# Idle TensorE slots filled with products that nothing reads, two joints reordered, stick-breaking values woven into the heads

## The chip, the cores and the metric

The kernel runs on one core of one Trainium2 chip. A core has five engines that run their own instruction streams in order and meet at semaphores: TensorE (PE in the rows), VectorE (DVE), ScalarE (ACT), GpSimd (POOL) and SyncE (SP), which here only issues transfers. The metric is the device time of one execution in microseconds. The time before is the median of three runs.

## The reference, cut to what matters

A first block of two layers works on 256 latent and 256 context tokens of width 1024 (the second layer on the latent tokens' output alone); a second block of two layers follows. Every stage begins with an RMS norm and a large product, so the pattern "norm, then product, then add to the residual" occurs throughout:

```
def rms_norm(x, g, eps=NORM_EPS):
    xf = x.astype(jnp.float32)
    y = xf * lax.rsqrt(jnp.mean(xf * xf, axis=-1, keepdims=True) + eps)
    return (y * g.astype(jnp.float32)).astype(x.dtype)
...
    def merge(h, fa, db, nc):
        gates = jax.nn.sigmoid(h @ w_g + b_gate)
        g_a, g_b, g_c = jnp.split(gates, N_BRANCH, axis=-1)
        return (g_a * (fa @ w_a) + g_b * (db @ w_b) + g_c * (nc @ w_c)) @ w_out
...
def _stick_breaking_attention(q, k, v):
...
        z = jnp.einsum('bthd,bshd->bhts', q[:, start:end], k[:, :end], preferred_element_type=jnp.float32) * scale
...
        log_1m = jnp.where(past, jax.nn.log_sigmoid(-z), 0.0)
        later = lax.cumsum(log_1m, axis=3, reverse=True) - log_1m
        w = jnp.where(past, jnp.exp(jax.nn.log_sigmoid(z) + later), 0.0)
        outs.append(jnp.einsum('bhts,bshd->bthd', w.astype(v.dtype), v[:, :end]))
...
def _stick_breaking_mixer(hn, w_qkv, w_out):
    B, S, _ = hn.shape
    qkv = (hn @ w_qkv).reshape(B, S, 3, SB_HEADS, HEAD_DIM)
    o = _stick_breaking_attention(qkv[:, :, 0], qkv[:, :, 1], qkv[:, :, 2])
    return o.reshape(B, S, SB_HEADS * HEAD_DIM) @ w_out
```

## The kernel before, in words

**Products.** Activations lie with the feature in the partitions and the tokens in the columns (512 columns in layer 0, 256 later). Each operand of a product is kept as a rounded high part and the rest, so one 128 by 128 weight tile costs three matmuls: weight high with activation high, weight high with activation low, weight low with activation high (L1241 to L1243, and for the first two tiles of a stage L1258, L1259, L1262). SyncE loads 1 MB slabs of weights into three buffers; ScalarE rounds a piece of 128x1024 to its high part (L1615, `WH`), VectorE subtracts to get the low part (L1944, `WL`); four pieces are in flight.

**Order.** A Python class `Plan` writes one list of steps; each engine runs its own steps in list order and waits on semaphores. `ahead()` puts the next pieces' high and low parts in the list; `tick`, `later` and `put_off` delay steps; banks and buffers are rings.

**Leads.** `lead` (L278) is the first product of a stage. It runs the eight feature tiles k outermost over two output tiles, so that each k can begin as its operand appears. After it came `ahead()`, then the two evictions.

**Norms.** `NormPlan` (L901) serves mix0, ffn0, mix1 and ffn1: a square per tile (ACT L1636), its column sums by a product with ones (PE L1309), the root (ACT L1681, L1684), then per k the normalised tile (DVE L1997, ACT L1692), its high part (ACT L1696) and low part (DVE L2002), which the next lead reads. `EarlyNorm` (L952) serves the other norms: it takes unnormalised tiles, adds the squares up on GpSimd (L1184), sums once on TensorE (L1315, L1317) and takes the root (L1665, L1668) while products already run. At ffn1_norm0 the adds are 512 columns wide.

**Merge.** `merged` marks the end of the three gated branches; ScalarE and VectorE then write the merged activations' high and low parts (L1818, L2103), and the `w_out` lead follows. Its two evictions (DVE L2132) and the squares behind them are "the joint" here.

**Stick-breaking (L717 to L763).** Queries and keys of group 0, then the values of all four groups, then eight units of two heads. A unit is `sb1` (scores, L1431), on ACT an absolute value, exponential and logarithm (L1844 to L1850), on DVE L2203 to L2210; three ticks later `sb2` (running sums by products, L1441 to L1443), DVE and ACT taking turns (L2215, L1855, L2217); three ticks later `sb3` (weights times values, L1455) and its copies (`sb_o`, L1859, L2221). The projections of query and key groups 1 to 3 are woven between the units. The lead of `sb_out` follows all units.

Of the kernel before, what the change touches and what calls it, by code (L numbers as in the profile page):

```python
# [10 lines left out]
ALU = mybir.AluOpType  # L11
# [134 lines left out]
class Plan:  # L146
# [110 lines left out]
    def gemm(self, name, w, col0, ncols, T, src, ready, ev, kt=8, k0=0, width=256, fine=True, x=None, hook=None, lead=False):  # L257
        g = Gemm(name, kt, T, src, ready, ev, x)
        self.lag = hook is not None
        for c in range(0, ncols, width):  # L260
            per = PIECE // (kt * 128)
            s = self.slab(w, k0, kt, col0 + c, width, [(0, kt, i * 128, (i + per) * 128) for i in range(0, width // 128, per)])
            if lead and c == 0:
                yield from self.lead(g, s, (0, 1), hook)
                continue
# [12 lines left out]
    def lead(self, g, s, ns, hook=None):  # L278
# [41 lines left out]
    def gemm_tok(self, name, w, col0, ncols, tiles, src, ready, ev, fine=True, x=None):  # L320
        self.lag = False
        g = Gemm(name, 8, 256, src, ready, ev, x)
        for c in range(0, ncols, 256):
            s = self.slab(w, 0, 8, col0 + c, 256, [(0, 4, 0, 256), (4, 8, 0, 256)])
            ps = [self.piece(s, 0), self.piece(s, 1)]
            for i, tt in enumerate(tiles):
# [9 lines left out]
                if fine or end:  # L336
                    yield

# [122 lines left out]
    def layer(self, l, nrm):  # L461
# [18 lines left out]
        self.finish(self.gemm(("u", l), w_in, 0, 512, T, ("A", T), ready, "u", lead=True))  # L480
# [115 lines left out]
        for k in range(8):  # L596
            self.add("yh", (l, k), n=T)
        nrm = NormPlan(self, f"ffn{l}", T)
        self.finish(self.gemm(("w_out", l), ("w_out", l), 0, 1024, T, ("B", 0), lambda k: ("yh", l, k), "res", x=(l, 2), hook=nrm, lead=True))
# [93 lines left out]
    def every(self):  # L693
# [28 lines left out]
        def sb_qk(j):  # L722
            yield from self.gemm(("sbq", j), wq, 256 * j, 256, T, ("A", T), ready, "sbq", x=2 * j, lead=j == 0)
# [4 lines left out]
        self.finish(self.gemm_tok(("sbv",), wq, 2048, 1024, range(2), "A", ready, "sbv"))  # L728
        sbo = {}
# [13 lines left out]
        def sb2(i, ts):  # L743
# [6 lines left out]
            def out():  # L750
                b, ls = self.banks.take(), (ts[0][1], ts[1][1])
                self.add("sb3", (i,), b=b, t=ls)
                for s in ls:
                    self.ys.give(s, ("sb_pv", i))
# [8 lines left out]
        self.finish(self.gemm(("sb_out",), ("sb_out", 0), 0, 1024, T, ("B", 0), lambda k: ("sbo", k), "res_add", hook=nrm, lead=True), False)  # L763
# [49 lines left out]
        def ns_q(j):  # L813
            yield from self.gemm(("nsq", j), win, 256 * j, 256, T, ("A", T), ready, "nsq", x=2 * j, lead=j == 0)
# [67 lines left out]
        for v in range(19):  # L882
# [10 lines left out]
        self.flush()  # L893
        self.root_was = [("ns_graw",)] + [("hn_root", ("nsq", 3), i) for i in range(2)]
        nrm = EarlyNorm(self, "ffn2_norm1", "ffn2_norm1")
        self.finish(self.gemm(("nsa_out",), ("nsa_out", 0), 0, 1024, T, ("B", 0), lambda k: ("nso", k // 2), "res_add", hook=nrm, lead=True), False)
# [1647 lines left out]
```

## Time and profile before

| | us |
|---|---|
| median of three runs | 2738.38 (2737.7 to 2739.89) |
| profiled execution, its own time | 2741.68 |
| its span, first to last instruction | 2739.9 |
| TensorE busy / VectorE / ScalarE / GpSimd | 2569.3 / 1558.0 / 1224.5 / 169.3 |
| mean granted clock of TensorE | 0.968 of full |

The granted clock has two levels in this trace, full (2.4 GHz) and half (1.2 GHz). "Idle before" in brackets behind a row is the time for which the engine stood still before it, with the instruction that ended the wait. In the timeline rows a matmul's length overlaps the next one's start, so the cost of one in a train is the distance between starts. A product of two fp32 operands is recorded as two matmuls.

### The profile page before, as it was taken

The numbers are of one execution on the slowest core, as the hardware profiler recorded it, in microseconds if no ns is written. First come the engines' busy times: TensorE is split into PE (matmuls) and PEld (weight loads), VectorE is DVE, ScalarE is ACT, GpSimd is POOL, SyncE is SP. The second block draws the span as 40 slices with busy tenths as digits, with TensorE's granted clock in tenths as the row PEclk, the third lists the DMA queues.
The fourth block names the chain that finished last, engine by engine and source line by source line (L and its number), as shares of the span: only waits on it lengthen the run. The fifth ranks groups of instructions, "written<-read, shape, count | busy, mean of one in ns | idle before, by whom it ended". The sixth has DMA issues, their size and how long they took to land.

```text
span 2739.9 us, 42203 instructions
## 1 busy us (share of the span) xinstructions
PE 2569.3 (94%) x17840; PEld 2266.3 (83%) x17840; DVE 1558.0 (57%) x2666; ACT 1224.5 (45%) x2026; POOL 169.3 (6%) x219
## 2 busy tenths in 40 slices
PE   5988799999999999999999999999899999988999
PEld 3865587777777776878889999998799999986999
DVE  2233335544565555454658877666666675766665
ACT  4234334433333334354546565455544543555543
POOL 0000000000000000000000011010100100025100
PEclk8998999999999999999999999999999999999999
DMA  7223432221354443232444555553255455440564
GB/s 237 85 85 123 146 108 82 75 91 62 127 181 139 154 139 123 93 116 93 131 146 161 186 170 194 185 185 124 96 194 188 150 193 198 161 135 1 185 200 139
DMA packets 337387, 382.12 MB, mean 139 GB/s; under 512 B 7408, under 2 KB 301296, under 8 KB 337200
## 3 DMA queue, kind: packets, MB, share of 16 engines
q1 hardware_dynamic: 334656, 370.37, 41.3%
q0 software_dynamic: 2544, 9.06, 1.1%
q8 instruction: 141, 2.31, 0.4%
q14 instruction: 46, 0.38, 0.0%
HBM read 378.36 MB, written 1.05 MB: 138 GB/s over the span
## 4 chain that ended last, share of the span: by engine, by line
PE 82%; ACT 7%; DVE 6%; DMA 2%; issue 1%; POOL 1%; SPq 0%; POOLq 0%; ACTq 0%; DVEq 0%
PE PS L1241 22%; PE PS L1243 21%; PE PS L1242 21%; ACT WH L1615 2%; DVE WL L1944 2%; PE PS L1278 1%; PE PS L1279 1%; PE PS L1280 1%; PE PS L1291 1%; DMA RAWB<-in_w_in 1%; PE PS L1258 1%; PE PS L1376 1%; PE PS L1259 1%; PE PS L1369 1%; PE PS L1262 1%
## 5 line engine op out<-in xcount | busy, mean ns | idle before, releaser
L1944 DVE TENSOR_TENSOR WL<-RAWB,WH 128x1024 fp32r<-128x1024 f32 (+2 forms) x613 | 736.0, 1209 | 604.7 <-ACT WH L1615 603.0
L1241 PE MATMUL PS<-AH,WH 128*128 128x256 f32 (+1 forms) x2912 | 912.1, 313 | 6.0 <-DVE WL L1944 6.0
L1243 PE MATMUL PS<-AH,WL 128*128 128x256 f32 (+1 forms) x2912 | 900.7, 309 | 0.0
L1242 PE MATMUL PS<-AL,WH 128*128 128x256 f32 (+1 forms) x2912 | 898.8, 309 | 0.0
L1615 ACT ACTIVATE WH<-RAWB 128x1024 fp32r<-128x1024 f32 (+2 forms) x613 | 625.8, 1034 | 358.8 <-PE PS L1243 171.0
L1241 PEld LDWEIGHTS PS<-AH,WH 128*128 128x128 f32 x2912 | 550.9, 189 | 61.5 <-issue 22.6
L1242 PEld LDWEIGHTS PS<-AL,WH 128*128 128x128 f32 x2912 | 551.8, 190 | 29.9 <-issue 0.8
L1243 PEld LDWEIGHTS PS<-AH,WL 128*128 128x128 f32 x2912 | 551.2, 189 | 30.6
L1241 PE MATMUL PS<-BH,WH 128*128 128x256 f32 (+1 forms) x1440 | 454.9, 316 | 0.8 <-DVE WL L1944 0.8
L1243 PE MATMUL PS<-BH,WL 128*128 128x256 f32 (+1 forms) x1440 | 442.5, 307 | 0.0
L1242 PE MATMUL PS<-BL,WH 128*128 128x256 f32 (+1 forms) x1440 | 441.2, 306 | 0.0
L1241 PEld LDWEIGHTS PS<-BH,WH 128*128 128x128 f32 x1440 | 273.1, 190 | 32.0 <-issue 14.0
L1242 PEld LDWEIGHTS PS<-BL,WH 128*128 128x128 f32 x1440 | 273.7, 190 | 16.0 <-issue 3.1
L1243 PEld LDWEIGHTS PS<-BH,WL 128*128 128x128 f32 x1440 | 273.0, 190 | 14.3
L2132 DVE SCALAR_TENSOR_TENSOR H<-PS,MOD,H 128x256 f32<-128x256 f32 x168 | 72.9, 478 | 87.6 <-PE PS L1243 76.9
L1740 ACT ACTIVATE F<-PS,PV 128x512 f32<-128x512 f32 (+1 forms) x88 | 58.4, 666 | 134.4 <-PE PS L1243 134.4
L1278 PE MATMUL PS<-WH,AH 128*128 128x256 f32 x352 | 99.3, 282 | 0.0
L1279 PE MATMUL PS<-WL,AH 128*128 128x256 f32 x352 | 98.3, 279 | 0.0
L1280 PE MATMUL PS<-WH,AL 128*128 128x256 f32 x352 | 98.2, 279 | 0.0
L2139 DVE SCALAR_TENSOR_TENSOR F<-PS,PV,F 128x255 f32<-128x255 f32 x132 | 63.0, 477 | 61.8 <-ACT F L1740 61.5
L1151 POOL DMA_DIRECT2D BI<-in_nab x16 | 11.4, 712 | 1272.3 <-DVE BL L2022 686.1
L2162 DVE SCALAR_TENSOR_TENSOR H<-PS,H 128x256 f32<-128x256 f32 x192 | 77.6, 420 | 18.7 <-PE PS L1243 16.4
(313 smaller groups left out, 2794.0 us busy)
## 6 DMA issues: line engine op xcount, KB each, us to landing
RAWB<-in_f_in SPq DMA_DIRECT2D x88, 1024.0 KB, 5.2
RAWB<-in_w_in SPq DMA_DIRECT2D x52, 1024.0 KB, 5.1
RAWB<-in_w_ada SPq DMA_DIRECT2D x48, 1024.0 KB, 5.4
RAWB<-in_w_up SPq DMA_DIRECT2D x44, 1024.0 KB, 5.2
RAWB<-in_f_out SPq DMA_DIRECT2D x40, 1024.0 KB, 5.1
RAWB<-in_w_down SPq DMA_DIRECT2D x20, 1024.0 KB, 5.4
RAWB<-in_sb_qkv SPq DMA_DIRECT2D x12, 1024.0 KB, 5.2
RAWB<-in_w_out SPq DMA_DIRECT2D x8, 1024.0 KB, 5.1
```

The lines of the kernel that those rows point to most:

```text
L1241: pe.matmul(out, h, xh[:, 0:T], start=k == 0, stop=False)
L1242: pe.matmul(out, h, xl[:, 0:T], start=False, stop=False)
L1243: i = pe.matmul(out, l, xh[:, 0:T], start=False, stop=k == g.kt - 1)
L1278: pe.matmul(out, h, wh, start=k == 0, stop=False)
L1279: pe.matmul(out, h, wl, start=False, stop=False)
L1280: i = pe.matmul(out, l, wh, start=False, stop=k == 7)
L1615: act.activation(c.part("WH", p), c.raw(p.slab)[:, k0:k1, c0:c1], ACT.Copy).then_inc(up("hi", ("hi", p.p)), 1)
L1740: act.activation(c.wide(s.t, g), b[:, 0:T], ACT.Identity, bias=c.sm(f"conv_b{l}", n, 1), scale=c.sm(f"conv_w{l}", 44 + n, 1)).then_inc(up( ...
L1944: dve.tensor_tensor(c.part("WL", p), c.raw(p.slab)[:, k0:k1, c0:c1], c.part("WH", p).bitcast(F32), ALU.subtract).then_inc(up("lo", ("lo", ...
L2132: t = stt(x, b[:, q * 256:q * 256 + 256], c.mod(l, part, n, q), x, ALU.mult, ALU.add)
L2139: stt(x[:, a + 1:e], b[:, a:e - 1], c.sm(f"conv_w{l}", n, 1), x[:, a + 1:e], ALU.mult, ALU.add).then_inc(up("vec", ("upb", g.name, n, q)), 1)
L2162: stt(x, b[:, 0:256], 0.5, x, ALU.mult, ALU.add).then_inc(up("vec", ("ev", g.name, n)), 1)
```

## The change

**Products of constants.** A step `busy` issues fp32 products of ones with a 128x256 block of constants into a bank that nothing reads: eight behind each root of mix0, ffn0 and mix1, four behind that of ffn1, five and three ahead of the `w_out` leads of layers 0 and 1, five behind the root of mix_norm1. In all 41.

**Joints.** A lead with a hook (`w_out` twice, `sb_out`, `nsa_out`) no longer puts the next weight pieces directly behind itself.

**Leads in parts.** The leads of `sb_out` and `nsa_out` are cut: `sb_out` runs k = 0 to 5 before the last units end, `nsa_out` runs k = 0 to 5 before its last two steps.

**Stick-breaking.** Only group 0 of the values comes before the heads; groups 1 to 3 are woven in with the query and key groups.

**Smaller parts.** The squares of mix0 use the two-slot ring of the other norms, shared with the rows of the modulation, instead of the ring of four. At ffn1_norm0 the adds 4, 5 and 6 run on VectorE.

```
@@ lead
-        self.add("mm_lead", n=ns, b=bs, g=g, p=ps)
+        for x in parts:
+            self.add("mm_lead", n=ns, b=bs, g=g, p=ps, x=x)
         for j in range(2):
             self.done(ps[j])
-        self.ahead()
+        if not hook:
+            self.ahead()
@@ new
+    def busy(self, n, *id):
+        b = self.banks.take()
+        self.add("busy", id, n=n, b=b)
+        self.banks.give(b, ("busy",) + id)
@@ merged
+        self.busy(5 if T == 512 else 3, "merged", l)
         nrm = NormPlan(self, f"ffn{l}", T)
@@ NormPlan
-        self.ring = plan.tmps if name == "mix0" else plan.sqs
...
+            plan.busy(8 if self.T == 512 else 4, self.name)
@@ EarlyNorm.sum
+        if name == "mix_norm1":
+            plan.busy(5, name)
@@ stick-breaking
-        self.finish(self.gemm_tok(("sbv",), wq, 2048, 1024, range(2), "A", ready, "sbv"))
-        sbo = {}
+        def sb_v(j):
+            yield from self.gemm_tok(("sbv", j), wq, 2048 + 256 * j, 256, range(2), "A", ready, "sbv", x=256 * j)
+            values.append(j)
+        done, values = [], []
+        self.finish(sb_v(0))
...
+                while i // 2 not in values:
+                    next(fill)
...
-        fill = itertools.chain(sb_qk(1), sb_qk(2), sb_qk(3))
-        self.weave(self.run_units(range(8), sb1), fill, 8, 13)
+        fill = itertools.chain(*(f(j) for j in range(1, 4) for f in (sb_qk, sb_v)))
+        self.weave(self.run_units(range(8), sb1), fill, 8, 18, False)
+        def sb_end():
+            k = 0
+            while self.put_off:
+                n = len(done)
+                self.tick()
+                if n > k:
+                    yield k, n
+                    k = n
+            yield k, 8
@@ nsa
+        def ns_end():
+            yield 0, 6
+            for v in range(17, 19):
+                step(v)
+            self.flush()
+            yield 6, 8
@@ engines
+def on_vector(s):
+    return s.x == 512 and s.id[1] > 3
...
-        elif s.kind == "sqadd":
+        elif s.kind == "sqadd" and not on_vector(s):
...
+        elif kind == "busy":
+            for f in s.b.was:
+                on.wait_ge(*at(*f))
+            for _ in range(s.n):
+                t = pe.matmul(c.bank(s.b)[:, 0:256], ones, c.m["CC"][:, 0:256], start=True, stop=True)
+            t.then_inc(up("acc", ("busy",) + id), 1)
```

ScalarE at the `w_out` lead of layer 0, before: `BH` is the merged activations' high part, `WH` the weight pieces, `SQ` the squares of the joint.

```order
L1818 ACTIVATE BH<-Y 128x512 x8
L1615 ACTIVATE WH<-RAWB 128x1024 x3
L1630 ACT_TABLE_LOAD
L1636 ACTIVATE SQ<-H 128x512 x3
L1615 ACTIVATE WH<-RAWB 128x1024
```

The same place in the changed kernel, where all lines below the insertions have larger numbers:

```order
L1866 ACTIVATE BH<-Y 128x512 x8
L1663 ACTIVATE WH<-RAWB 128x1024
L1678 ACT_TABLE_LOAD
L1684 ACTIVATE SQ<-H 128x512 x2
L1663 ACTIVATE WH<-RAWB 128x1024 x2
```

Two of the three pieces have moved from ahead of the table load to behind the second square.

ScalarE at the start of the stick-breaking heads, before: `F<-PS,LM` is the eviction of values, L1835 the table load of the heads.

```order
L1750 ACTIVATE F<-PS,LM 128x256 x2
L1615 ACTIVATE WH<-RAWB 128x1024 x2
L1750 ACTIVATE F<-PS,LM 128x256 x2
L1835 ACT_TABLE_LOAD
L1844 ACTIVATE Y<-PS 128x384 x2
L1847 ACTIVATE Y<-Y 128x384 x2
L1850 ACTIVATE Y<-Y 128x384 x2
L1615 ACTIVATE WH<-RAWB 128x1024 x2
```

In the changed kernel:

```order
L1798 ACTIVATE F<-PS,LM 128x256 x2
L1883 ACT_TABLE_LOAD
L1892 ACTIVATE Y<-PS 128x384 x2
L1895 ACTIVATE Y<-Y 128x384 x2
L1898 ACTIVATE Y<-Y 128x384 x2
L1663 ACTIVATE WH<-RAWB 128x1024 x3
L1903 ACTIVATE Y<-Y 128x384 x2
```

One group's two evictions stand ahead of the heads instead of four groups' eight; the other six lie between the heads' exponentials.

TensorE at the end of the heads, before: the last `sb2`, two `sb3`, and the first product of the `sb_out` lead.

```order
L1441 MATMUL PS<-TMP,CX 128x256
L1442 MATMUL PS<-TMP,CC 128x128
L1443 MATMUL PS<-TMP,CX 128x128
L1455 MATMUL PS<-Y,F 64x256 x2
L1457 MATMUL PS<-Y,F 64x128 x2
L1455 MATMUL PS<-Y,F 64x256 x2
L1457 MATMUL PS<-Y,F 64x128 x2
L1258 MATMUL PS<-BH,WH 128x256
```

In the changed kernel, from the last product of the lead's first part:

```order
L1304 MATMUL PS<-BH,WL 128x256
L1489 MATMUL PS<-TMP,CX 128x256
L1490 MATMUL PS<-TMP,CC 128x128
L1491 MATMUL PS<-TMP,CX 128x128
L1489 MATMUL PS<-TMP,CX 128x256
L1490 MATMUL PS<-TMP,CC 128x128
L1491 MATMUL PS<-TMP,CX 128x128
L1503 MATMUL PS<-Y,F 64x256 x2
L1505 MATMUL PS<-Y,F 64x128 x2
L1300 MATMUL PS<-BH,WH 128x256
```

The first 36 of the lead's 48 products stand ahead of the last `sb2`, and six more between the last two `sb3`.

## Rows read from the trace of the kernel before

**Rows 1.** The page: engines' busy time; the chain that ended last.
```profile
PE 2569.3 (94%) x17840; PEld 2266.3 (83%) x17840; DVE 1558.0 (57%) x2666; ACT 1224.5 (45%) x2026; POOL 169.3 (6%) x219
...
PE 82%; ACT 7%; DVE 6%; DMA 2%; issue 1%; POOL 1%; SPq 0%; POOLq 0%; ACTq 0%; DVEq 0%
```

**Rows 2.** Windows: stretches in which the granted clock (PEclk) was half.
```profile
core 0: us, PE busy (x) PEld busy (x) DVE busy (x) ACT busy (x) POOL busy (x), PEclk, DMA share, GB/s
...
661.77:668.60 6.83, 4.91 (x12) 3.88 (x13) 6.78 (x16) 6.67 (x15) 0.00 (x0) 0.50 0.01 2
...
1405.87:1409.28 3.41, 3.41 (x18) 3.41 (x17) 2.34 (x5) 1.41 (x3) 0.00 (x0) 0.50 0.00 0
...
1440.01:1446.83 6.82, 4.75 (x22) 4.79 (x23) 6.02 (x15) 6.21 (x15) 0.00 (x0) 0.50 0.00 1
1641.39:1648.22 6.83, 5.09 (x12) 3.03 (x13) 3.82 (x4) 4.55 (x7) 2.60 (x4) 0.50 0.52 137
...
2426.46:2433.29 6.83, 5.43 (x23) 4.80 (x24) 1.17 (x3) 0.72 (x2) 0.00 (x0) 0.50 0.47 154
```

**Rows 3.** Timeline, TensorE at the first `w_out` lead.
```profile
start us, us, engine line op out<-in xcount [idle before <-releaser]
...
599.86 0.47 PE L1258 MATMUL PS<-BH,WH 128*128 128x512 f32 x1 [3.09 <-DVE BL L2103]
```

**Rows 4.** Timeline of the first joint: ScalarE, VectorE, TensorE.
```profile
612.04 2.00 ACT L1615 ACTIVATE WH<-RAWB 128x1024 fp32r<-128x1024 f32 x2 [8.57 <-PE PS L1262]
614.06 1.28 ACT L1630 ACT_TABLE_LOAD   x1
615.36 1.15 ACT L1636 ACTIVATE SQ<-H 128x512 f32<-128x512 f32 x2
...
612.04 1.66 DVE L2132 SCALAR_TENSOR_TENSOR H<-PS,MOD,H 128x256 f32<-128x256 f32 x4 [7.09 <-PE PS L1262]
...
616.04 1.12 PE L1309 MATMUL PS<-SQ,CC 128*128 128x512 f32 x2 [3.35 <-ACT SQ L1636]
```

**Rows 5.** Waits of TensorE from 1402 to 1416: total, times, longest.
```profile
PE PS L1309 <- ACT SQ L1636: 3.5, 1, 3.5
PE PS L1258 <- ACT BH L1818: 2.6, 1, 2.6
```

**Rows 6.** Timeline, TensorE and VectorE behind the root of ffn0.
```profile
663.69 0.77 PE L1258 MATMUL PS<-AH,WH 128*128 128x512 f32 x1 [4.88 <-ACT TMP L1692]
...
672.98 0.69 DVE L2002 TENSOR_TENSOR AL<-TMP,AH 128x512 fp32r<-128x512 f32 x1 [0.77 <-ACT AH L1696]
...
676.81 0.39 PE L1262 MATMUL PS<-AH,WL 128*128 128x512 f32 x1
677.04 0.39 PE L1241 MATMUL PS<-AH,WH 128*128 128x512 f32 x1
```

**Rows 7.** Timeline of ffn1_norm0's sum: GpSimd and TensorE.
```profile
1635.29 7.78 POOL L1184 TENSOR_TENSOR GT<-GT,SQ 128x512 f32<-128x512 f32 x5 [0.76 <-ACT SQ L1656]
...
1643.13 2.07 PE L1315 MATMUL PS<-GT,CC 128*128 128x512 f32 x2 [4.90 <-POOL GT L1184]
```

**Rows 8.** Stick-breaking: windows of the values and of the heads; TensorE's longest waits there.
```profile
1841.72:1863.75 22.03, 22.03 (x197) 21.90 (x195) 8.80 (x9) 10.07 (x14) 0.00 (x0) 1.00 0.58 183
1863.75:1950.49 86.74, 70.02 (x512) 62.31 (x513) 58.17 (x112) 44.26 (x86) 0.00 (x0) 0.89 0.26 85
...
PE PS L1431 <- DVE F L2172: 9.1, 2, 6.0
```

**Rows 9.** Timeline, TensorE at the root of mix_norm1.
```profile
2423.15 0.59 PE L1315 MATMUL PS<-GT,CC 128*128 128x256 f32 x2
2423.58 0.59 PE L1317 MATMUL PS<-SQ,CC 128*128 128x256 f32 x2
2427.86 1.22 PE L1495 MATMUL PS<-SQ,CC 128*128 128x256 f32 x2 [3.68 <-ACT SQ L1873]
```

**Rows 10.** Timeline, TensorE at the first lead of the program and near the end of nsa.
```profile
54.17 0.77 PE L1258 MATMUL PS<-AH,WH 128*128 128x512 f32 x1 [6.80 <-ACT TMP L1692]
...
2521.51 0.65 PE L1590 MATMUL PS<-F 15*64 15x256 f32 x4 [2.35 <-ACT Y L1913]
```

More of the change, by code:

```diff
@@ L263, in gemm @@
             if lead and c == 0:
-                yield from self.lead(g, s, (0, 1), hook)
+                yield from self.lead(g, s, (0, 1), hook, lead)
                 continue
@@ L479, in layer @@
         self.add("c256", (l,))
-        self.finish(self.gemm(("u", l), w_in, 0, 512, T, ("A", T), ready, "u", lead=True))
+        self.finish(self.gemm(("u", l), w_in, 0, 512, T, ("A", T), ready, "u", lead=((0, 8),)))
         def tok_dft(g):
@@ L722, in sb_qk @@
         def sb_qk(j):
-            yield from self.gemm(("sbq", j), wq, 256 * j, 256, T, ("A", T), ready, "sbq", x=2 * j, lead=j == 0)
+            yield from self.gemm(("sbq", j), wq, 256 * j, 256, T, ("A", T), ready, "sbq", x=2 * j, lead=() if j else ((0, 8),))
             yield from self.gemm(("sbk", j), wq, 1024 + 256 * j, 256, T, ("A", T), ready, "sbk", x=2 * j)
@@ L813, in ns_q @@
         def ns_q(j):
-            yield from self.gemm(("nsq", j), win, 256 * j, 256, T, ("A", T), ready, "nsq", x=2 * j, lead=j == 0)
+            yield from self.gemm(("nsq", j), win, 256 * j, 256, T, ("A", T), ready, "nsq", x=2 * j, lead=() if j else ((0, 8),))
             self.later(6, lambda: have.__setitem__(j, True))
@@ L881, in every, with step @@
         next(fill)
-        for v in range(19):
+        def step(v):
             if v < 16:
@@ L892, in every @@
             self.tick()
-        self.flush()
+        def ns_end():
[4 more added lines that the diff above has]
+            yield 6, 8
+        for v in range(17):
+            step(v)
         self.root_was = [("ns_graw",)] + [("hn_root", ("nsq", 3), i) for i in range(2)]
         nrm = EarlyNorm(self, "ffn2_norm1", "ffn2_norm1")
-        self.finish(self.gemm(("nsa_out",), ("nsa_out", 0), 0, 1024, T, ("B", 0), lambda k: ("nso", k // 2), "res_add", hook=nrm, lead=True), False)
+        self.finish(self.gemm(("nsa_out",), ("nsa_out", 0), 0, 1024, T, ("B", 0), lambda k: ("nso", k // 2), "res_add", hook=nrm, lead=ns_end()), False)
         self.finish(self.swiglu(2, 1, "ffn2_norm1", None, "f21"))
@@ L921, in sum @@
         plan.add("sqsum", (self.name,), n=(i, k), b=self.b, t=q, x=self.T)
-        self.ring.give(q, ("sqsum", self.name, i))
+        plan.sqs.give(q, ("sqsum", self.name, i))
         if i == 7:
@@ L1247, in tensor_program @@
             out = [c.bank(b)[:, 0:T] for b in s.b]
-            for b in s.b:
+            for b in s.b if s.x[0] == 0 else []:
                 for f in b.was:
                     on.wait_ge(*at(*f))
-            for k in range(8):
+            for k in range(*s.x):
                 xh, xl = c.operand(g.src, k)
@@ L1308, in tensor_program @@
             on.wait_ge(*at("sq", id[0], k))
-            pe.matmul(c.bank(s.b)[:, 0:s.x], ones, (c.tmp if id[0] == "mix0" else c.sq)(s.t)[:, 0:s.x], start=i == 0, stop=i == 7).then_inc(
+            pe.matmul(c.bank(s.b)[:, 0:s.x], ones, c.sq(s.t)[:, 0:s.x], start=i == 0, stop=i == 7).then_inc(
                 up("acc", ("sqsum", id[0], i)), 1)
+        elif kind == "busy":
[4 more added lines that the diff above has]
+            t.then_inc(up("acc", ("busy",) + id), 1)
         elif kind == "xsum":
@@ L1977, in vector_program @@
                 up("vec", ("xlo",) + id), 1)
+        elif kind == "sqadd" and on_vector(s):
+            name, i = id
+            acc = c.gt(s.b)[:, 0:s.x]
+            on.wait_ge(*at("xsq", name, i))
+            on.wait_ge(*at("sqadd", name, i - 1))
+            dve.tensor_tensor(acc, acc, c.sq(s.t)[:, 0:s.x], ALU.add).then_inc(up("vec", ("sqadd", name, i)), 1)
         elif kind == "xroot" and s.x[1]:
```

17 lines of the change are left out of this document (9 added, 8 removed).

## The prediction

> **What bounds the kernel now.** I read the page's busy times and its chain of waits first, then the stretches of half clock, then the timeline around each wait that the change touches. TensorE is busy for 94% of the span and makes 82% of the chain [rows 1]. So a microsecond is won where TensorE stands still, or where it runs at half clock behind such a standstill. Both show at every place touched. At ffn0 it waits 4.88 us for the first normalised tile [rows 6], and 6.83 us at half clock begin inside that wait [rows 2]. At the first `w_out` lead it waits 3.09 us for the merged activations' low part [rows 3], at the joint behind that lead 3.35 us for the first square [rows 4]. In layer 1 the same two waits are 2.6 and 3.5 us [rows 5], and a stretch of 3.41 us at half clock begins about a microsecond after the first ended [rows 2]. The reader should see the pattern: a wait of two or more microseconds, then a stretch of half clock of one or two times 3.41 us. A product-bound stretch loses half of its busy time.
>
> **The change part by part.** The sum is made against the profiled execution's own 2741.68 us, that is the span and 1.8 us around it. The median is 3.3 us below that, and I carry the saving over to the median unchanged.
>
> *Price of a filler.* One fp32 product over 256 columns is two records. Two such sums start 0.43 us apart at full clock [rows 9], so a filler costs 0.43 us at full and an estimated 0.86 us at half. Eight take 3.44 us, five 2.15, four 1.72, three 1.29. They fit into the waits of 4.88, 3.09, 3.68 and 2.6 us, leaving 1.44, 0.94, 1.53 and 1.3 us empty. They shorten no wait; they can only keep the clock. If the clock is down when they start, eight take 6.9 us, which overruns the 4.88 us by 2.0.
>
> *First merged lead, both layers.* If the clock stays up, about 1.6 us of each 3.41 us stretch is won back, being a little under half: 3.2 us together, between 0 and 3.4.
>
> *Joints.* Before, ScalarE does two weight pieces (2.00 us), the table load (1.28), then the squares, from 615.36 [rows 4]. Now the table load comes first, and as it waits for nothing it runs under the lead. The square then waits only for the first tile's eviction, two of the four VectorE instructions of 1.66 us: ready at about 612.04 + 0.83 + 0.04 = 612.91, against 615.36. That wins 2.45 us. In layer 1 the eviction is one instruction a tile; of the 3.5 us wait, I take 2.85 away by the same reckoning. The wait that is left is below 1 us, so each stretch of half clock behind it should go too: twice 1.6. Together 8.5. The weight pieces come later by up to 2 us, but two pieces are already split at that moment and cover two tiles of 24 products, so I cost the delay at nothing. If it were seen, it would be up to 2.0 a joint.
>
> *Root of ffn0.* At full clock the stretch of 661.77 would give back half of its 4.91 us busy, 2.45 [rows 2]. But the last low part is only done at 672.98 + 0.69 = 673.67 [rows 6], and six products at 0.23 us (676.81 to 677.04) follow it: 675.04, against 677.04 now. So 2.0. *Root of mix1:* the same chain feeds products half as long, which wait for it anyway: 0. *Root of ffn1:* half of 4.75 us [rows 2] is 2.4, the operands' chain takes part of it back, I take 1.4 (0 to 2.4).
>
> *ffn1_norm0.* GpSimd's five adds take 7.78 us, 1.56 each, and TensorE waits 4.90 us for the last [rows 7]. Three of the six adds go to VectorE; a two-input instruction of that size on it takes 0.69 [rows 6]. Three times 0.87 is 2.6 us off the wait, leaving 2.3. That is about where the clock fell elsewhere, so of the 2.5 us that the stretch costs (half of 5.09, [rows 2]) I take 1.7. Together 4.3, between 2.0 and 5.1.
>
> *Stick-breaking.* Values take 22.03 us of pure TensorE work ahead of the heads. Then the heads take 86.74 us, in which TensorE is idle for 16.7, 9.1 of it for two waits for scores' operands [rows 8]. Three quarters of the values, 16.5 us, move into the heads, 36 of the lead's 48 products ahead of the last running sums, six more between the last outputs. The most it can win is what is idle, 16.7 us, and part of the half-clock excess (granted clock 0.89 over the heads). But the idle time is one unit's chain through VectorE and ScalarE in turns, and VectorE is busy for 58.17 of the 86.74 us already; the moved pieces add 7 us to it. I take half of the idle time, 8 us (below 0 to 18).
>
> *Root of mix_norm1.* The wait of 3.68 us keeps 1.53 empty; half of 5.43 us [rows 2, 9] is 2.7, of which I take 2.2.
>
> *nsa and mix0.* The cut `nsa_out` lead fills the wait of 2.35 us [rows 10], but those products had covered the copies of the last output, so that wait comes back behind. At mix0 each modulation row must now be turned before the next square has its buffer; the fillers at half clock take about the 6.80 us [rows 10] that stand empty. For each I take 0.5 us lost, between 2.4 won and 2.4 lost, the former wait being the nearest row.
>
> Sum: 3.2 + 8.5 + 2.0 + 0 + 1.4 + 4.3 + 8 + 2.2 − 1.0 = 28.6. Of this, 10.5 us rest on fillers or a shortened wait holding the clock (3.2 + 2.0 + 1.4 + 1.7 + 2.2). Since a microsecond or more stays empty at most of these places, I count three quarters of them, taking off 2.6: 26 us. That is 2715.7 for the profiled execution and 2738.38 − 26 = 2712 for the median.
>
> *A rule against it.* The trace shows the clock falling behind the 2.6 us wait of [rows 5]. The Trainium skill, "TensorE: Matmul & The Clock Gate", section "HAM oscillation — how this bites in real kernels", states that only longer idle gaps than this one bring the clock down. By that rule the falls behind 2.6 and 3.09 us would not come from the waits, and taking the waits away would leave the clock as it is; the row contradicts it here, and so I give the case below a small chance.
>
> **The rivals.**
> *A. The fillers don't hold the clock.* For it: most waits keep about a microsecond or more empty, and a filler waits for its bank's last reader, so it may start late. Against it: TensorE's work in these waits rises from nothing to more than half. The 8.8 us that hang on fillers (3.2 + 2.0 + 1.4 + 2.2) are gone; 28.6 − 8.8 = 19.8: 2718.6.
> *B. The values in the heads win nothing.* VectorE and ScalarE, in order, then carry both; TensorE's freed slots are where it waits for them. For it: every one of the long waits there is for VectorE. Against it: the values' own pieces are few. 26 − 8 = 18: 2720.4.
> *C. The clock falls for a cause other than these waits,* so that every term of clock is lost, also at the joints and at ffn1_norm0: 8.8 + 3.2 + 1.7 = 13.7. 28.6 − 13.7 = 14.9: 2723.5. The trace speaks against it: a fall behind every wait of two microseconds that I looked at.
> *D. The weave is better than half.* 16 us, nearly all the idle time, would give 26 + 8 = 34: 2704.
> *E. Slower.* Place: ScalarE's queue in the heads. Six evictions of values now stand between exponentials, and each waits for its TensorE group, a group being a quarter of 22.03 us over two tiles, 2.75 us each. If the queue stands still for each of six tiles, and the same again for the weight pieces that wait behind it, the heads lose up to 33 us in place of winning 8. The others win 18, so it turns to slower above 18 us of loss, 3.0 us a tile; at 33 the time is 2753. Against it: ScalarE is busy for only 44.26 of 86.74 us.
> That the change does not do what it says is A for the fillers and B for the heads.
>
> **How the numbers follow.** Forecast 0.47, A 0.15, B 0.17, C 0.05, D 0.10, E 0.06. The forecast's own range is 2706 to 2718. Leaving out 0.2 at the ends, I give 2698 to 2727: it holds D, A, B and C, and not the most of E. About 0.2% (5.5 us) is what a measurement of this kernel tells from no change. Only E, in half of its range, is slower by more; a mixture of losses may end within. Faster 0.90, same 0.05, slower 0.05.
>
> **What would show it.** *Fillers:* no stretch of half clock right behind the roots of ffn0, ffn1 and mix_norm1 and behind the merged activations, with the waits as long as before, less the fillers. If half clock stays, A or C. *Joints:* the first square within 1 us of the lead's end, and the table load under the lead. *ffn1_norm0:* TensorE's wait at 2.3 us and two fewer microseconds of GpSimd adds behind one another. *Heads:* from the first value product to the end of the lead some 8 us less; a wait of TensorE for scores' operands below the 6.0 us. If it is longer, E. *nsa, mix0:* within 0.5 us of before. The forecast would be wrong by most if the heads' stretch did not shorten, since it is the largest term and the one least supported by rows.

## The result and the profile after

The changed kernel takes 2706.81 us (median of four, 2704.24 to 2712.47), beside 2739.14 us for the kernel before on the same chip (2737.7 to 2746.05). The ratio is 0.988, with an interval of 0.9861 to 0.9899. Run once more beside the experiments, the same kernel takes 2707.69 us, ratio 0.9885 (0.9868 to 0.9901). The medians differ by 32.3 us. The forecast was 2712 us, 26 us less than before; its direction and its range held, but several terms did not, and this part is about those.

The profiled execution takes 2707.78 us with a span of 2706.0, that is 33.9 us less than before, at a mean granted clock of 0.98 instead of 0.968. The page, engines' busy time and the chain that ended last:

```profile
PE 2568.7 (95%) x17922; PEld 2264.6 (84%) x17922; DVE 1557.0 (58%) x2669; ACT 1224.9 (45%) x2026; POOL 164.7 (6%) x216
...
PE 83%; ACT 6%; DVE 6%; DMA 2%; issue 1%; POOL 1%; SPq 0%; ACTq 0%; POOLq 0%; DVEq 0%
```

TensorE has 82 records more than in [rows 1], the 41 fp32 products of two records each, and yet is busy for 0.6 us less. By the 0.43 us of [rows 9] these fillers are an estimated 17.6 us of work, so the other work is busy for about 18 us less, won back from stretches at half clock. That is about half of the 33.9 us; the other half is idle time that is gone and not merely filled with products.

**Stage by stage.** The same instruction of VectorE or ScalarE is sought in both traces, and the difference of its start times is followed through the program. The table gives how far that difference moved over each stage, against the profile of before (microseconds, negative is shorter). "No fillers", "mended fillers" and "best" are the experiments 1, 2 and 9 below; "before, again" is a second profile of the kernel before (experiment 11).

| stage (start and end in the time of before) | predicted | after | after, again | no fillers | mended fillers | best | before, again |
|---|---|---|---|---|---|---|---|
| start, mix0 (0 to 110) | +0.5 | −4.68 | −3.44 | −5.69 | −3.22 | −3.18 | +0.16 |
| `w_out` layer 0 (560 to 630) | −5.65 | −5.58 | −5.57 | −4.00 | −5.58 | −5.56 | −1.58 |
| root of ffn0 (630 to 700) | −2.0 | −0.59 | −0.59 | −0.85 | −1.67 | −1.81 | −0.63 |
| root of mix1 (1030 to 1130) | 0 | +1.22 | +1.22 | +0.01 | −0.01 | 0.00 | −0.02 |
| `w_out` layer 1 (1380 to 1425) | −6.05 | −5.88 | −5.89 | −5.88 | −6.09 | −5.88 | 0.00 |
| root of ffn1 (1425 to 1470) | −1.4 | −1.01 | −1.00 | −0.13 | −1.34 | −1.33 | −0.61 |
| ffn1_norm0 (1628 to 1650) | −4.3 | −3.03 | −3.04 | −3.03 | −3.04 | −3.03 | −0.02 |
| stick-breaking (1800 to 1975) | −8 | −9.81 | −9.66 | −8.89 | −9.42 | −10.88 | −2.76 |
| root of mix_norm1 (2415 to 2450) | −2.2 | −2.57 | −2.55 | +0.11 | −2.58 | −2.53 | +0.12 |
| nsa's end (2512 to 2545) | +0.5 | +1.37 | −0.08 | +1.54 | +1.52 | +0.04 | +0.05 |
| sum of these | −28.6 | −30.56 | −30.60 | −26.81 | −31.43 | −34.16 | −5.29 |
| rest of the span, not touched | 0 | −3.3 | −2.3 | +2.3 | +1.4 | −3.4 | +5.6 |

The reader should see three things. Between the two profiles of the changed kernel seven of the ten touched stages repeat within 0.1 us. Between the two profiles of the kernel before they do not: where a stretch of half clock comes once and not the other time, `w_out` of layer 0, ffn0, ffn1 and the stick-breaking stage are shorter by 0.6 to 2.8 us without any change, so the gains there are smaller by as much against the second profile (stick-breaking 7.0 us and not 9.8, ffn0 nothing). And the stages that the change does not touch move by several microseconds together, which no term of the prediction holds.

**Where the terms came out.** Timeline, TensorE and ScalarE at the first `w_out` lead and its joint, then TensorE at the first lead of the program, behind the root of ffn0, at ffn1_norm0 and at the root of mix_norm1; columns as in [rows 3]:

```profile
592.76 2.32 PE L1357 MATMUL PS<-CC 128*128 128x256 f32 x10
596.02 0.47 PE L1300 MATMUL PS<-BH,WH 128*128 128x512 f32 x1 [0.94 <-DVE BL L2157]
...
599.65 1.28 ACT L1678 ACT_TABLE_LOAD   x1
...
607.51 0.63 ACT L1684 ACTIVATE SQ<-H 128x512 f32<-128x512 f32 x1 [6.58 <-DVE H L2186]
...
608.20 1.13 PE L1351 MATMUL PS<-SQ,CC 128*128 128x512 f32 x2 [0.94 <-ACT SQ L1684]
...
51.07 0.77 PE L1300 MATMUL PS<-AH,WH 128*128 128x512 f32 x1 [4.49 <-ACT TMP L1740]
...
649.24 3.62 PE L1357 MATMUL PS<-CC 128*128 128x256 f32 x16
...
652.95 0.91 ACT L1740 ACTIVATE TMP<-TMP,MOD 128x256 f32<-128x256 f32 x2 [2.16 <-PE PS L1357]
655.50 0.47 PE L1300 MATMUL PS<-AH,WH 128*128 128x512 f32 x1 [2.65 <-ACT TMP L1740]
...
1614.11 2.28 DVE L2031 TENSOR_TENSOR GT<-GT,SQ 128x512 f32<-128x512 f32 x3 [1.26 <-POOL GT L1226]
1616.45 1.63 PE L1363 MATMUL PS<-GT,CC 128*128 128x512 f32 x2 [2.56 <-DVE GT L2031]
...
2384.60 2.32 PE L1357 MATMUL PS<-CC 128*128 128x256 f32 x10
2388.43 0.70 PE L1543 MATMUL PS<-SQ,CC 128*128 128x256 f32 x2 [1.52 <-ACT SQ L1921]
```

The joint is as forecast: the table load lies under the lead, the first square starts at 607.51 behind the eviction, and TensorE's wait fell from 3.35 us [rows 4] to 0.94. Ahead of the lead five fillers leave 0.94 of the 3.09 us [rows 3]. At mix_norm1, 1.52 of 3.68 us [rows 9] stay empty, as reckoned. At ffn1_norm0 three adds on VectorE take 2.28 us, and the wait is 2.56 instead of 4.90 [rows 7]. Against the reckoning is the root of ffn0: ScalarE's first scaled tile waits 2.16 us, and what it waits for is the filler (L1357). Windows of the changed kernel (columns: stretch, length, busy time and count of PE, PEld, DVE, ACT, POOL, then granted clock, DMA share, GB/s):

```profile
592.76:618.00 25.24, 23.36 (x98) 18.07 (x97) 12.20 (x19) 11.25 (x16) 0.00 (x0) 1.00 0.13 42
...
1819.00:1911.00 92.00, 86.59 (x696) 79.99 (x694) 64.70 (x116) 53.04 (x97) 0.00 (x0) 0.98 0.38 124
1911.00:1920.00 9.00, 6.04 (x26) 4.87 (x27) 3.13 (x8) 2.34 (x6) 0.00 (x0) 0.50 0.02 5
2384.00:2394.00 10.00, 8.48 (x61) 7.68 (x60) 5.57 (x7) 5.47 (x9) 0.00 (x0) 1.00 0.51 173
```

The clock is full (1.00, 2.4 GHz) behind the first merged activations and behind mix_norm1, where before it fell to half [rows 2]. In the heads TensorE is now busy for 86.59 of 92 us instead of 70.02 of 86.74 [rows 8], at a granted clock of 0.98 instead of 0.89; most of the half clock that is left lies in the 9 us at their end. TensorE's longest waits in the heads, then those at nsa's end (total, times, longest):

```profile
PE PS L1300 <- DVE BL L2275: 3.2, 2, 2.3
PE PS L1503 <- DVE Y L2271: 2.3, 1, 2.3
PE PS L1489 <- DVE TMP L2264: 2.0, 1, 2.0
PE PS L1479 <- DVE F L2226: 0.7, 1, 0.7
...
PE PS L1638 <- ACT Y L1961: 2.3, 1, 2.3
PE PS L1300 <- DVE BL L2423: 1.4, 1, 1.4
```

The 9.1 us for scores' operands [rows 8] have shrunk to 0.7 (L1479); what heads the list is the second part of the cut lead (L1300), which now waits for the copies of the last outputs. At nsa's end likewise, the former wait of 2.35 us [rows 10] is still there, and 1.4 us for the lead's second part has been added.

### The profile page after: what moved, and what is told of

Same layout as the page of the kernel before. It is cut to its first block, busy times and chain, and to the rows that moved or that the text cites. A ratio compares the mean times of both kernels' runs of the same rounds, so it can differ in the third digit from the quotient of the medians.

```text
span 2706.0 us, 42375 instructions
## 1 busy us (share of the span) xinstructions
PE 2568.7 (95%) x17922; PEld 2264.6 (84%) x17922; DVE 1557.0 (58%) x2669; ACT 1224.9 (45%) x2026; POOL 164.7 (6%) x216
## 4 chain that ended last, share of the span: by engine, by line
PE 83%; ACT 6%; DVE 6%; DMA 2%; issue 1%; POOL 1%; SPq 0%; ACTq 0%; POOLq 0%; DVEq 0%
PE PS L1283 22%; PE PS L1285 21%; PE PS L1284 21%; DVE WL L1992 2%; PE PS L1333 2%; ACT WH L1663 2%; PE PS L1320 2%; PE PS L1321 1%; PE PS L1322 1%; DMA RAWB<-in_w_in 1%; PE PS L1351 1%; PE PS L1424 1%; PE PS L1300 1%; PE PS L1417 1%; PE PS L1399 1%
```

## The experiments

Experiments 1 to 5, 9 and 10 were timed in rounds with the kernel before, the others run once. 1 to 4 shared one chip, 5 to 8 a second, 9 to 11 a third. Diffs are against the changed kernel.

**1. Fillers left out.** The steps `busy` are gone, and nothing else.

```
 def busy(self, n, *id):
-        b = self.banks.take()
-        self.add("busy", id, n=n, b=b)
-        self.banks.give(b, ("busy",) + id)
+        return
```

> The changed kernel without its 41 products of constants; all else as changed. Theory: the fillers keep the clock at the first merged leads (1.6 us each), at the root of ffn1 (1.0) and of mix_norm1 (2.6), but at ffn0 and mix1 they also hold up ScalarE: its first scaled tile there waits 1.22 us for the last filler, because the fillers are counted ahead of the mark that frees the activations' buffer. So without them: half clock is back at all these places, first merged leads +1.6 each, ffn0 +0.6, mix1 -1.2, ffn1 +1.0, mix_norm1 +2.6; the whole 6.2 us slower than the changed kernel, about 2713 us. Rival: the fillers do not hold the clock, the falls came and went by chance; then the stages stay within 0.3 us except ffn0 and mix1, which become 1.2 us shorter, and the whole is about 2704 us.

Measured: 2717.17 us (2702.55 to 2720.89, five), ratio 0.9913 (0.9884 to 0.9943). The intervals of this ratio and of the changed kernel's overlap, so the stages have to tell: fillers are worth 1.6 us at `w_out` of layer 0, 0.9 at ffn1, 2.7 at mix_norm1, nothing at `w_out` of layer 1, and they cost 0.3 at ffn0 and 1.2 at mix1. That is 3.7 us together; of the 9.4 us between the two spans (2715.4 and 2706.0) 5.6 lie in stages that the change does not touch (last row of the table), and what start, stick-breaking and nsa differ by cancels. Without them, TensorE's wait at the second merge, the window there, then the wait and window at mix_norm1:

```profile
PE PS L1298 <- ACT BH L1864: 2.6, 1, 2.6
...
1386.00:1400.00 14.00, 10.69 (x87) 10.26 (x86) 7.61 (x16) 8.70 (x16) 0.00 (x0) 1.00 0.46 152
...
PE PS L1541 <- ACT SQ L1919: 3.7, 1, 3.7
...
2393.80:2400.60 6.80, 5.69 (x24) 5.03 (x25) 0.88 (x3) 0.72 (x2) 0.00 (x0) 0.50 0.48 154
```

Behind the wait of 3.7 us the clock falls, as before [rows 2], and fillers hold it. The first merged lead and the roots of ffn0 and ffn1 show the same: all three profiles without fillers (this one and both of before) have half clock at these four places; of the ten with fillers none has it at the lead, at ffn1 or at mix_norm1, and three have it at ffn0. At mix1 the fillers do not hold it: nine of the ten have half clock there all the same, eight of them for 3.41 us where those without fillers have 6.83. But behind the same 2.6 us of [rows 5] it does not fall here, while it did in both profiles of before. So a wait of that length makes a fall possible, not certain. The Trainium skill, "TensorE: Matmul & The Clock Gate", section "HAM oscillation — how this bites in real kernels", gives a rule that warns of longer idle gaps than this only; the run here agrees with it and [rows 5] with [rows 2] does not, so taken as a bound the page's rule is not the whole condition.

**2. Fillers behind the mark.** The mark on which ScalarE's first scaled tile waits is taken ahead of the fillers; TensorE's order is the same.

```
@@ NormPlan.sum
-            plan.busy(8 if self.T == 512 else 4, self.name)
@@ NormPlan.split
         plan.mark("A" + name)
+        plan.busy(8 if self.T == 512 else 4, self.name)
```

> The changed kernel with the fillers of the four full norms issued at the same place of TensorE's order, but counted behind the mark that frees the activations' buffer instead of ahead of it. Theory of the held-up mark: ScalarE's first scaled tile no longer waits for TensorE at ffn0 and mix1, each of these two stages becomes 1.2 us shorter (drift against before at ffn0 -1.8 instead of -0.6, at mix1 0.0 instead of +1.2); whole 2.4 us faster than the changed kernel. Rival: TensorE's fillers themselves are what the lead waits for; then nothing moves, since they are as many and in the same place.

Measured: 2707.42 us (2698.38 to 2711.75, four), ratio 0.9884 (0.9856 to 0.9913). The total does not tell; the stages do. ScalarE and TensorE at the root of ffn0:

```profile
653.55 0.91 ACT L1740 ACTIVATE TMP<-TMP,MOD 128x256 f32<-128x256 f32 x2 [0.95 <-DVE TMP L2051]
...
656.10 0.47 PE L1300 MATMUL PS<-AH,WH 128*128 128x512 f32 x1 [1.43 <-ACT TMP L1740]
```

The 2.16 us before the first scaled tile are 0.95, and TensorE's wait is 1.43 instead of 2.65: 1.22 us less, the amount by which mix1 had become longer. Both stages give it back (ffn0 −1.67 instead of −0.59, mix1 −0.01 instead of +1.22). The cause is shown: the fillers are counted on TensorE's semaphore ahead of the mark, so ScalarE waited for products that nothing reads.

**3. The squares of mix0 in the old ring of four.**

```
@@ NormPlan
+        self.ring = plan.tmps if name == "mix0" else plan.sqs
-        q = self.plan.sqs.take()
+        q = self.ring.take()
...
-        plan.sqs.give(q, ("sqsum", self.name, i))
+        self.ring.give(q, ("sqsum", self.name, i))
```

> The changed kernel with the squares of the first norm in their own ring of four buffers again, as before. Theory: with two shared buffers TensorE's turns and sums follow one another later, the slabs' buffers are freed later, and the first slabs of the next product no longer compete with the last slab of the modulation: that slab's wait of 3.49 us went, and the first norm ended 4.7 us earlier. So here the wait of about 3.5 us for the modulation's last slab is back and the first lead starts about 4 us later; whole 4 us slower than the changed kernel, all behind it unchanged. Rival: the loads at the start simply vary from run to run; then the first lead starts within 1 us of the changed kernel's.

Measured: 2709.19 us (2702.49 to 2717.03), ratio 0.9896 (0.9869 to 0.9923). TensorE at the last modulation row and ScalarE at the root behind it, with the window of half clock, in the kernel before; row and root in the changed kernel; then row, root and first lead here:

```profile
38.52 1.94 PE L1291 MATMUL PS<-RAWB,SC 128*32 128x256 f32 x16 [3.49 <-DMA RAWB<-in_w_ada]
45.91 0.69 ACT L1681 ACTIVATE RS<-PS,EPS 128x512 f32<-128x512 f32 x1 [4.28 <-PE PS L1309]
37.13:57.61 20.48, 12.29 (x44) 8.23 (x45) 9.68 (x23) 10.03 (x18) 0.00 (x0) 0.50 0.58 188
...
38.44 1.07 PE L1333 MATMUL PS<-RAWB,SC 128*32 128x256 f32 x16
43.16 0.69 ACT L1729 ACTIVATE RS<-PS,EPS 128x512 f32<-128x512 f32 x1 [1.22 <-PE PS L1351]
...
37.52 1.52 PE L1334 MATMUL PS<-RAWB,SC 128*32 128x256 f32 x16 [2.81 <-DMA RAWB<-in_w_ada]
44.49 0.69 ACT L1730 ACTIVATE RS<-PS,EPS 128x512 f32<-128x512 f32 x1 [4.30 <-PE PS L1352]
...
52.75 0.77 PE L1301 MATMUL PS<-AH,WH 128*128 128x512 f32 x1 [3.81 <-DVE AL L2057]
```

With the old ring a wait of 2.81 us for the last slab is back, and the lead starts 1.7 us later than the 51.07 of the changed kernel, not the 4 us expected. The theory had the mechanism wrong: the last row begins at the same time before and after the change (38.52 and 38.44), so no earlier slab wins the time. What differs is the clock. Before, it is half from 37.13 us, inside the wait of 3.49 us, and the root follows 7.39 us behind the row's start; in the changed kernel TensorE comes to that row without a wait and at full clock, and the root follows 4.72 us behind. Here it follows 6.97 us behind. All ten profiles with the shared ring, that without fillers among them, have 4.7, so the ring wins 2.3 to 2.7 us at this place. The rest of the start varies: the last row begins between 37.1 and 38.5 us from run to run, and of the ten profiles with the shared ring five have a stretch of 3.41 us at half clock behind the first lead (the stage then gains 3.2 to 4.0 us) and five do not (4.7 to 6.0 us).

**4. All values ahead of the heads again**, with the cut lead and the rest of the change in place.

```
-        self.finish(sb_v(0))
+        for j in range(4):
+            self.finish(sb_v(j))
...
-        fill = itertools.chain(*(f(j) for j in range(1, 4) for f in (sb_qk, sb_v)))
-        self.weave(self.run_units(range(8), sb1), fill, 8, 18, False)
+        fill = itertools.chain(sb_qk(1), sb_qk(2), sb_qk(3))
+        self.weave(self.run_units(range(8), sb1), fill, 8, 13, False)
```

> The changed kernel with the values of all four groups ahead of the heads again and only queries and keys woven in; the lead of sb_out stays cut into the heads' end. Theory: of the 9.8 us that the stick-breaking stage won, the weave of the values is the larger part, about 6, since the units' chains through VectorE and ScalarE lie bare without it; the cut lead is the rest, about 4. So this stage +6 us against the changed kernel. Rival: the cut lead won nearly all, because the last units had nothing beside them; then +2 us or less.

Measured: 2715.61 us (2711.76 to 2719.82), ratio 0.9924 (0.99 to 0.9947). The stage loses 6.3 of its 9.7 us (−3.46). The wait for scores' operands of [rows 8] is back:

```profile
PE PS L1480 <- DVE F L2227: 9.2, 2, 6.1
...
PE PS L1301 <- DVE BL L2276: 2.7, 1, 2.7
```

So about two thirds of the stage's gain against the first profile of before are values woven into the heads. The other 3.5 us are not shown to be a gain of the order at their end: the second profile of before, with nothing changed, is already at −2.76.

**5. Both leads' order at nsa mended**, with the fillers of experiment 2: the two last steps are issued and flushed first, and the lead runs whole.

```
-        def ns_end():
-            yield 0, 6
-            for v in range(17, 19):
-                step(v)
-            self.flush()
-            yield 6, 8
-        for v in range(17):
+        for v in range(19):
...
+        self.flush()
-        ... hook=nrm, lead=ns_end()), False)
+        ... hook=nrm, lead=((0, 8),)), False)
```

> The changed kernel with two parts mended: the fillers of the full norms counted behind the mark, and the lead of nsa_out whole again behind the last outputs. Theory: the cut nsa lead gives the wait for the last output's copies back (1.42 us ahead of its k = 6) and fills nothing, since the wait of 2.34 us lies ahead of its first part; so with the lead whole this stage is 1.4 us shorter than in the changed kernel, ffn0 1.1 and mix1 1.2 us, whole 3.7 us faster than the changed kernel, about 35 us faster than before. Rival: the first part did shorten something, and taking it back costs as much; then the nsa stage stays at +1.4 against before.

Measured: 2704.84 us (2704.4 to 2711.02), ratio 0.9875 (0.9853 to 0.9898). The total does not tell it from the changed kernel. nsa's end comes to +0.05 instead of +1.37, though a stretch of 3.41 us at half clock is there as in the changed kernel. Of the nine profiles with the cut lead all have the wait of 1.4 us; eight have that stretch too and lose 1.1 to 1.5 us, and the ninth, the changed kernel's second, is at full clock from 2470 to 2500 and comes to −0.08. So with the stretch the cut costs 1.1 to 1.5 us. In the ninth the missing stretch hides the cost, and no run has the whole lead at full clock to compare.

**6. Next weight pieces back at the joints.**

```
-        if not hook:
-            self.ahead()
+        self.ahead()
```

> The changed kernel with the next weight pieces put directly behind the leads again at w_out (twice), sb_out and nsa_out; fillers and all else as changed. Theory: ScalarE's two pieces and the table load stand ahead of the first square again; each w_out stage gets 2.45 and 2.85 us of wait back, and half clock behind it (1.6 each): w_out stage of layer 0 drifts by -1.6 instead of -5.6 against before, that of layer 1 by -2.0 instead of -5.9. Rival: the fillers ahead of the lead already keep the clock at the joint; then only the waits come back, -3.1 and -3.0. sb_out and nsa_out within 0.5 us.

Measured: 2722.5 us, one run. ScalarE and TensorE at the first joint, and the window behind the second merge:

```profile
605.52 2.00 ACT L1662 ACTIVATE WH<-RAWB 128x1024 fp32r<-128x1024 f32 x2 [6.97 <-PE PS L1303]
607.54 1.28 ACT L1677 ACT_TABLE_LOAD   x1
608.83 1.15 ACT L1683 ACTIVATE SQ<-H 128x512 f32<-128x512 f32 x2
...
609.51 1.24 PE L1350 MATMUL PS<-SQ,CC 128*128 128x512 f32 x2 [3.35 <-ACT SQ L1683]
...
1405.70:1412.50 6.80, 5.93 (x26) 5.75 (x26) 0.54 (x1) 1.11 (x3) 0.00 (x0) 0.50 0.50 154
```

The order of [rows 4] is back, with the same 3.35 us wait. Layer 0 loses 4.0 us (−1.59 instead of −5.58), which is the 2.45 + 1.6 of the prediction. Layer 1 loses 5.5 us (−0.40), as the stretch at half clock behind its wait is 6.8 us here and not the 3.41 of [rows 2]. One expectation missed: the stick-breaking stage, with the pieces back behind the lead of `sb_out`, comes to −11.55, 1.7 us shorter than in the changed kernel and not within 0.5. Its end has 6.83 us of half clock where the changed kernel has 10.24, so the clock can account for it; the order is not ruled out.

**7. All six adds of ffn1_norm0 on GpSimd again.**

```
 def on_vector(s):
-    return s.x == 512 and s.id[1] > 3
+    return False
```

> The changed kernel with all six adds of ffn1_norm0 on GpSimd again. Theory: TensorE's wait for the sum goes from 2.56 back to 4.9 us and this stage is 2.3 to 3.0 us longer; the half clock behind it is off the path, since the products behind the sum wait in their evictions for the root anyway, so it costs nothing more whether it falls for 3.4 or 6.8 us. Rival, as the prediction had it: the longer half clock costs another 1.7 us, together 4.3 or more.

Measured: 2710.17 us, one run. GpSimd and TensorE there:

```profile
1610.86 7.75 POOL L1226 TENSOR_TENSOR GT<-GT,SQ 128x512 f32<-128x512 f32 x5 [0.76 <-ACT SQ L1704]
...
1618.67 2.08 PE L1363 MATMUL PS<-GT,CC 128*128 128x512 f32 x2 [5.19 <-POOL GT L1226]
```

The stage is back at −0.03, with 7.75 us of adds as in [rows 7]. So the adds win 3.0 us. The clock shows no part in it: experiments 1 and 5 show no half clock at all at this place and win the same 3.03.

**8. The lead of `sb_out` whole**, behind all units.

```
+        self.flush()
-        ... hook=nrm, lead=sb_end()), False)
+        ... hook=nrm, lead=((0, 8),)), False)
```

> The changed kernel with the lead of sb_out whole behind all units, the values still woven in. With the values first again and the cut lead kept the stage lost 6.0 of its 9.4 us. Theory: the two parts add up, so that the cut lead is worth the other 3.4 us: +3.4 here. Rival: they fill the same idle slots (the tail of the heads), and the woven values have already covered most of the tail; then +1.5 us or less.

Measured: 2706.28 us, one run. Stick-breaking comes to −10.87, against −9.81 and −9.66 with the cut lead. So the cut does not win the 3.4 us expected, nor does it win anything that shows. That it costs 1.1 us is not shown: here the heads end with 6.8 us at half clock and in the changed kernel with 10.24, and experiment 6, cut lead and 6.83 us of half clock, is shorter still (−11.55).

**9. The mended parts together:** 2, 5 and 8.

> The changed kernel with three parts mended: fillers behind the mark, and both the nsa_out and the sb_out lead whole. Theory: 1.1 us at ffn0, 1.2 at mix1, 1.2 to 1.4 at nsa, and 1.0 at sb_out, where the whole lead runs its first products while the last outputs are copied: 4.5 us faster than the changed kernel, and about 36 us faster than before. Rival: the scatter of the clock at sb_out was all that the whole lead showed; then 3.6.

Measured: 2701.64 us (2699.52 to 2704.17, four), ratio 0.9863 (0.9848 to 0.9878). The changed kernel beside it takes 2707.69 (2706.5 to 2710.19): the ranges do not meet, and the version is 6.0 us shorter than the changed kernel by medians. By the table's stages it should be 3.6 us (34.16 − 30.60); the two profiled spans differ by 4.6 us, 1.1 of it in stages that neither touches, and what else the medians differ by is left open. TensorE's longest waits in stick-breaking, then at nsa's end:

```profile
PE PS L1485 <- DVE TMP L2260: 4.6, 2, 2.7
PE PS L1475 <- DVE F L2222: 2.4, 2, 1.7
PE PS L1499 <- DVE TMP L2267: 1.8, 1, 1.8
...
PE PS L1634 <- ACT Y L1957: 2.3, 1, 2.3
```

Neither list has a wait of the lead (L1300 of the changed kernel) any more: products held back to the end cover the copies.

**10 and 11. The two kernels once more.** What untouched stages do by themselves.

> The changed kernel itself once more, on the chip that also runs the kernel with three parts mended. Theory of the chance part: drift against the first profile of before within 0.4 us at both joints, at ffn0, mix1, mix_norm1 and nsa as in the first profile of the changed kernel, but different by several microseconds where trains of products ran at 113.3 ns apart in one profile and 117.8 in another (1480 to 1620, and the last stage). Rival: those two stages were moved by the change too; then they repeat.

> The kernel before, once more, for what varies without any change. Theory: the start varies by some microseconds (the wait for the modulation's last slab is not always 3.49 us), half clock comes or not behind the same waits, and the last stage runs at 117.8 ns a product like nearly all other profiles; so drift against the first profile of before of -3 to -6 us by the first lead and of +6 in the last stage. Rival: the first profile of before is typical; drift within 1 us throughout.

Measured: 2707.69 us for the changed kernel (above), 2742.02 for the kernel before, one run. The start of the kernel before repeats within 0.16 us where −3 to −6 was expected; its half clock comes and goes as expected, and the stages concerned move by 0.6 to 2.8 us (last column of the table). Windows of untouched stretches: the changed kernel's first profile,

```profile
1480.00:1520.00 40.00, 40.00 (x355) 40.00 (x354) 33.48 (x54) 24.87 (x38) 0.00 (x0) 1.00 0.56 186
```

its second,

```profile
1480.00:1520.00 40.00, 40.00 (x342) 40.00 (x341) 33.02 (x52) 23.91 (x35) 0.00 (x0) 1.00 0.55 181
```

the first profile of before,

```profile
2600.00:2640.00 40.00, 40.00 (x356) 40.00 (x355) 27.36 (x41) 19.68 (x27) 3.70 (x5) 1.00 0.59 196
```

and its second:

```profile
2600.00:2640.00 40.00, 40.00 (x342) 40.00 (x341) 25.41 (x37) 18.03 (x25) 3.98 (x6) 1.00 0.60 200
```

TensorE is busy for all of the 40 us, and the granted clock is 1.00 in all four, yet the number of products differs by 4%. This is where the untouched stages' −5.4 us (1480 to 1630, in the changed kernel's first profile and in experiment 7) come from, and the +6.8 us of the last stage (2555 to the end), which all other profiles show, the kernel before too against its own first profile.

## Why the prediction was right, and which steps failed

*The bound.* Right: the span shrank by 33.9 us, about half of it idle time of TensorE and half work that no longer runs at half clock. Rivals B, D and E are out by the table: the heads won 9.8 us, or 7.0 against the second profile of before, and not 0, 16 or a loss. C is out, since at three places half clock came in all profiles without fillers and in none of the ten with them (experiment 1). A is half true, place by place.

*Joints.* Right in place and size: −5.58 and −5.88 for merge and joint together, against −5.65 and −6.05, and experiment 6 takes out 4.0 in layer 0 as reckoned. In layer 0 the 1.6 us of clock hang on the execution: in the second profile of before the stretch behind the joint did not come, and the stage is 1.58 us shorter.

*Fillers ahead of the merged leads.* 1.6 in layer 0, right. In layer 1 no worth of theirs is shown: in the one profile without them the clock stayed up behind the same wait (experiment 1). The mended joint does not explain that, since before the change the clock fell at 1405.87 us [rows 2], ahead of the joint's wait; why it stayed up is open.

*Fillers behind the roots.* At mix_norm1 right (2.7 for 2.2), at ffn1 near (0.9 for 1.4). At ffn0 and mix1 the failed step is "They shorten no wait; they can only keep the clock": they lengthened one. I had counted who waits for TensorE's result, but not that in this kernel a mark waits for every instruction ahead of it; ScalarE's wait on the mark that frees the activations' buffer became a wait for the last filler, 1.22 us at each. This turned an expected 2.0 into 0.6 at ffn0 (1.7 with the mark mended) and 0 into a loss at mix1. Experiment 2 shows it. Apart from it, fillers do not always hold the clock: it fell in three of ten profiles at ffn0 and in nine at mix1. The *price of a filler* held: eight take 3.62 us (L1357 at 649.24) for 3.44.

*ffn1_norm0.* The wait shrank by 2.34 to the 2.56 us forecast within 0.3, and the stage won 3.0. The clock's 1.7 was wrong: the half clock went in some executions and stayed in others, with the same −3.03, so it cost nothing there. That the products behind the sum wait for other work anyway is argued, not shown.

*Stick-breaking.* Near, and partly by luck: 9.8 against the first profile of before and 7.0 against the second, for 8, and no more than "half of the idle time" stood behind the 8. By experiment 4 the woven values are worth 6.3, about 1.7 of which can be the clock, since that run has 3.4 us more of half clock in this stage. The cut lead, which the prediction counted as part of the gain, shows none (experiment 8); where the rest of the 9.8 comes from, apart from the clock, is open.

*nsa.* The step "the cut `nsa_out` lead fills the wait of 2.35 us" failed: that wait stayed at 2.3. The other half held, a wait came back behind the old one, of 1.4 us, so the loss was 1.4 for 0.5 in the first profile.

*mix0.* Wrong in sign: −4.68 and −3.44 for +0.5. The step "each modulation row must now be turned before the next square has its buffer" was priced as a loss. With the shared ring TensorE's wait for the last slab, 3.49 us before, is gone, and so is the half clock under that row and the sums behind it: 4.72 us from the row to the root for 7.39, and 6.97 with the old ring back (experiment 3). So 2.3 to 2.7 us are the ring's. The remainder, some 0.5 to 3.5 us, goes with when the last row can begin and with a half-clock stretch behind the first lead that five of the ten profiles have; what sets these is open.

*The sum.* Terms too large by 5.4 us (ffn0 1.4, mix1 1.2, ffn1_norm0 1.3, nsa 0.9, ffn1 0.4, the two merges 0.2) stand against terms too small by 7.4 (mix0 5.2, the heads 1.8, mix_norm1 0.4). So the stages gave 2.0 more than the 28.6; the quarter taken off for the clock, 2.6, was not needed, and untouched stages gave 3.3 in that execution. Together that is 7.9 above the 26, or 33.9. The total was near because errors of five microseconds cancelled, which is luck. The sum also has a slip: the 10.5 us said to rest on the clock leave out the joints' 3.2, which case C counts as clock.

## What to carry to other kernels

Before a filler is put on an engine, look which marks of that engine others wait on, and put it behind them: a product that nothing reads can still hold up the reader of the one before it. An idle slot is best filled with work that is needed (the values, 6.3 us) and next by moving what lies in the way (the joints, 4.0 and 5.5); fillers gave 0.9 to 2.7 us where they held the clock, and nothing that shows at `w_out` of layer 1 and at mix1. When a change is worth about one per cent, follow the start times of the same instructions through both traces, and profile the kernel before twice as well: untouched stages moved by five to seven microseconds between executions of one program, and touched ones by up to 2.8.

## What the runs showed of the hardware that was not expected

Trains of the same 128x256 products run at two spacings while the granted clock reads 1.00: from start to start 113.3 ns in the windows of 355 and 356 records and 117.8 ns in those of 342 (a window counts the records that reach into it, too). Which one a stretch has changes between executions of the same kernel (1480 to 1520 of the changed kernel, 2600 to 2640 of the kernel before); what sets it stays open. And the same wait of TensorE, 2.6 us ahead of the second `w_out` lead, was followed by half clock in both profiles of the kernel before and not in the one of the kernel without fillers.
